# A two-layer decoder step: value half of the gated MLP by token, expert pages freed by quarters, a seventh state buffer

## The chip, the core and the metric

The kernel runs on one core of one Trainium2 chip. The metric is the device time in microseconds of one execution, from the first instruction to the last; lower is better. The time before is the median of three runs, 1581.47 us (1578.85 to 1586.49). A profiled execution gives the rows that are read below.

## What is computed

One inference step over 256 prompt tokens and 32 sample tokens (8 requests of 4), so 288 tokens in all, in float32. Layer 0 mixes tokens with an mLSTM block (a matrix memory of 4 heads for each request), layer 1 with a gated MLP whose gate is a causal 128-token spatial product; each is followed by a mixture of 32 experts with two experts for each token. Cut to what matters here:

```python
# mLSTM, for each request b and head h (8 x 4 = 32 sample states, 512 x 512 each)
c_new = decay[..., None, None] * c_prev + jnp.einsum('bhld,bhlv->bhdv', wk, v)

# gated MLP of layer 1; x is normalised first
zz = jax.nn.gelu(x @ p['cmlp_w_in'][j] + p['cmlp_b_in'][j])   # 1024 -> 4096
u, v = jnp.split(zz, 2, axis=-1)                              # 2048 each
v = layer_norm(v, p['cmlp_ln_w'][j], p['cmlp_ln_b'][j])       # over the 2048 features
mixed = jnp.einsum('gts,bcsgd->bctgd', ws, vp) + bias         # over tokens, 8 groups
return (u * mixed) @ p['cmlp_w_out'][j] + p['cmlp_b_out'][j], v

# experts, for each of 32: 1024 -> 512 gate and up, 512 -> 1024 down
a = jnp.einsum('td,edf->tef', x, p['moe_w_gate'][i, g])
b = jnp.einsum('td,edf->tef', x, p['moe_w_up'][i, g])
hg = jax.nn.silu(a) * b * combine[:, g, :, None]
y = y + jnp.einsum('tef,efd->td', hg, p['moe_w_down'][i, g])
```

## The kernel before

The program is written out by hand, engine by engine, with semaphores; nothing reorders it. TensorE is fed by `pe`, VectorE by `dve`, ScalarE by `act`, and almost all transfers are issued in order by the SyncE queue, `sp`: a wait in that queue holds back every transfer behind it. The big SBUF tensor `arena` holds ten slots of 2 MB (`pool10`), of which six form the `ring` that the dense weights use. A float32 product shows as two TensorE instructions in the trace; a transpose shows as one.

**States.** The 32 sample states of 1 MB each are loaded (`load_state`, L343), updated in place by VectorE (L1848), and stored (L396). Six half slots of the ring hold them (`cview`). In the loop at L393 to L406, `sp` stores state q as soon as it is updated, then waits until state q - 1 has landed in HBM, and then loads state q + 5 into the place that became free. When no state is left to load, the freed slots take the weights of the next projection, `z` (`load_z`): `z0` after store 27, `z1` after store 29, `z2` after store 31. TensorE reads each state in L1299, updates it through L1308, and begins `z` (L974) when everything of the last head is done and `z0` has landed.

**Experts.** Each layer runs 8 quads of four experts, each quad in two halves of two experts. The weights are pages of 2 MB, 24 for each turn of two quads: `gate`, `gate`, `up`, `up`, `down`, `down`, four times (`load_page`, L448). Ten slots take them in the order of `PAGE_SLOT`. Pages 0 to 9 are loaded ahead of the first product; page n from 10 on reuses the slot of page n - 10 (of page n - 6 from 20 on) and waits until the product that read it is done. So pages 10 to 13 wait for the end of the first `gate_up` (L1400, semaphore `gu_mm` at 1), pages 14 and 15 for the first `outputs` (L1431, `y_mm` at 1), pages 16 to 19 for the second `gate_up` (`gu_mm` at 2), and so on. `quad` sets the order of TensorE: `gate_up`, `hidden`, `outputs`, the gather of the next quad (L1374), the second `gate_up`, `hidden`, `outputs`.

**Gated MLP.** `dense("in", ...)` computes 32 tiles of 128 features by 288 tokens (L974): 16 of the value half, then 16 of the u half, 8 products each. VectorE scales each by the norm of the token (`in_scaled`, L2088), ScalarE applies the gelu with the bias of the feature (L876). The value half is needed by token, so after tiles 5, 9, 13 and 17 TensorE transposes four tiles back (`v_by_token`, L1581), VectorE copies them and takes their statistics (`values`), and after tiles 20, 22 and 24 normalises them (`layer_norm`). The spatial products (`mix`, L1536 and L1538) start behind tile 27, three for each tile, and VectorE gates u with them (`mixed`). The spatial weights are transposed once (L1570).

## Time and profile before

| | us |
|---|---|
| median of 3 runs | 1581.47 |
| lowest, highest | 1578.85, 1586.49 |
| the profiled execution | 1583.27 |
| its span, first to last instruction | 1581.5 |
| TensorE matmul busy in it | 1315.9 (83%) |
| VectorE, ScalarE busy | 510.5 (32%), 191.5 (12%) |
| moved by DMA | 532.97 MB, mean 337 GB/s |

The span falls into stretches: the up projection until about 95 us, the states until 290, `z` and `down` until 430, routing and the experts of layer 0 until 890, the gated MLP and its output until 1110, routing and the experts of layer 1 until the end. A busy share over the whole span mixes them; each stretch has its own limit. The chain of waits tells, going back from the last instruction, which work released which; the timeline of the SyncE queue tells when each transfer was issued, and the table of transfers how long it took to land.

### The profile page before, as it was taken

To read this page: it belongs to the slowest core of one execution; us is meant where nothing else is said; L and a number is where in the kernel's file an instruction comes from. 1 tells how busy PE (TensorE), PEld (TensorE's weight loads), DVE (VectorE), ACT (ScalarE), POOL (GpSimd) and SP (SyncE) were. 2 spreads that over 40 slices of the span, in tenths; PEclk is the share of its full clock that TensorE was granted. 3 is DMA by queue.
4 is the path that set the end of the run, shared out by engine and by line. 5 is a ranking of instruction groups with operands and counts; after the bars stand their busy time and mean duration, and the time that the engine had idled before them with its cause. 6 is when DMAs were issued, how large, how long until landed. Compare 5 with 4: busy or idle time off the path is not lost.

```text
span 1581.5 us, 18294 instructions
## 1 busy us (share of the span) xinstructions
PE 1315.9 (83%) x7577; PEld 734.7 (46%) x7579; DVE 510.5 (32%) x1187; ACT 191.5 (12%) x425; POOL 39.3 (2%) x78
## 2 busy tenths in 40 slices
PE   9999999999999486586585899999997757756766
PEld 6664443577654242242242577777543323323323
DVE  5757776432042022022021133630422212211212
ACT  2252221200110000000000312100200000000001
POOL 4120000000000000000000000000000000000000
PEclk9999999999999897898898999999998888888889
DMA  7228999958549999999999955361599999999996
GB/s 238 104 93 331 388 400 393 335 178 342 203 180 428 428 427 428 428 428 428 428 428 425 395 207 198 128 257 62 209 429 426 428 428 428 427 430 428 426 430 281
DMA packets 78120, 532.97 MB, mean 337 GB/s; under 512 B 6697, under 2 KB 24297, under 8 KB 43945
## 3 DMA queue, kind: packets, MB, share of 16 engines
q1 hardware_dynamic: 75112, 527.14, 81.9%
q10 hardware_dynamic: 2312, 4.20, 0.7%
q8 instruction: 52, 0.85, 0.2%
q0 software_dynamic: 624, 0.62, 0.2%
q14 instruction: 20, 0.16, 0.0%
HBM read 492.45 MB, written 39.49 MB: 336 GB/s over the span
## 4 chain that ended last, share of the span: by engine, by line
PE 58%; DMA 33%; DVE 5%; issue 2%; SPq 1%; ACT 1%; DVEq 0%
DMA arena<-in_moe_w_up 29%; PE bank L974 24%; PE bank L1400 10%; PE bank L1431 5%; PE bank L1444 3%; DMA arena<-in_moe_w_down 2%; PE bank L1374 2%; PE bank L1115 2%; PE bank L1299 1%; PE bank L1308 1%; PE bank L1408 1%; DVE arena L1848 1%; SPq L448 1%; PE bank L1100 1%; DMA out_C_s<-arena 1%
## 5 line engine op out<-in xcount | busy, mean ns | idle before, releaser
L1400 PE MATMUL bank<-arena,hT 128*32 128x512 f32 x2048 | 270.0, 687 | 193.8 <-DMA arena<-in_moe_w_up 183.6
L974 PE MATMUL bank<-hT,arena 128*128 128x288 f32 x1024 | 259.1, 411 | 0.0
L1400 PEld LDWEIGHTS bank<-arena,hT 128*32 128x32 f32 x2048 | 75.8, 124 | 375.7 <-issue 375.2
L974 PEld LDWEIGHTS bank<-hT,arena 128*128 128x128 f32 x1024 | 192.8, 191 | 56.8 <-issue 2.4
L1998 DVE TENSOR_TENSOR arena<-arena,bank 64x512 f32<-64x512 f32 x32 | 22.1, 692 | 545.9 <-ACT arena L837 545.9
L1431 PE MATMUL bank<-arena 128*32 128x512 f32 x1024 | 133.2, 664 | 21.6 <-DVE arena L2002 20.6
L1374 PE MATMUL bank<-arena 128*128 128x128 f32 (+1 forms) x768 | 136.8, 308 | 1.2 <-DVE arena L1973 0.9
L974 PE MATMUL bank<-arena 128*128 128x288 f32 x512 | 127.9, 409 | 0.0
L1374 PEld LDWEIGHTS bank<-arena 128*128 128x128 f32 (+1 forms) x768 | 104.3, 187 | 43.4 <-issue 12.7
L974 PEld LDWEIGHTS bank<-arena 128*128 128x128 f32 x512 | 96.1, 190 | 30.8 <-issue 3.5
L837 ACT ACTIVATE arena<-bank 64x512 f32<-64x512 f32 x32 | 18.8, 588 | 744.4 <-PE bank L1400 744.4
L1848 DVE SCALAR_TENSOR_TENSOR arena<-arena,bank 128x512 f32<-128x512 f32 x128 | 86.6, 740 | 34.7 <-PE bank L1308 34.6
L1431 PEld LDWEIGHTS bank<-arena 128*32 128x32 f32 x1024 | 38.9, 120 | 90.1 <-issue 89.8
L1444 PE MATMUL bank<-arena 128*128 128x288 f32 x240 | 65.9, 418 | 4.7 <-DVE xT L2031 3.9
L1991 DVE TENSOR_TENSOR hT<-bank,gpk 128x512 f32<-128x512 f32 x32 | 22.1, 691 | 117.3 <-PE bank L1374 117.3
L1444 PEld LDWEIGHTS bank<-arena 128*128 128x128 f32 x240 | 43.1, 189 | 33.3 <-issue 13.4
L1408 PE MATMUL bank<-ident,arena 64*128 64x64 f32 x256 | 35.6, 279 | 24.0 <-DVE arena L1998 22.9
L2031 DVE TENSOR_TENSOR xT<-xT,bank 128x288 f32<-128x288 f32 x120 | 52.0, 452 | 10.4 <-PE bank L1444 6.4
L1408 PEld LDWEIGHTS bank<-ident,arena 64*128 64x128 f32 x256 | 31.0, 188 | 44.1 <-DVE arena L1998 37.4
L1299 PE MATMUL bank<-arena 128*32 128x512 f32 x256 | 35.9, 633 | 5.0 <-DMA arena<-in_state_mlstm_C 4.9
L2088 DVE TENSOR_TENSOR arena<-bank,arena 128x288 f32<-128x288 f32 x32 | 14.6, 456 | 70.0 <-PE bank L974 70.0
L1308 PE MATMUL bank<-arena 32*128 32x512 bf16 x128 | 35.1, 392 | 0.6 <-ACT arena L716 0.4
(367 smaller groups left out, 991.0 us busy)
## 6 DMA issues: line engine op xcount, KB each, us to landing
arena<-in_moe_w_gate SPq DMA_DIRECT2D x64, 2048.0 KB, 29.2
arena<-in_moe_w_up SPq DMA_DIRECT2D x60, 2048.0 KB, 33.4
arena<-in_moe_w_down SPq DMA_DIRECT2D x60, 2048.0 KB, 25.4
arena<-in_state_mlstm_C SPq DMA_DIRECT2D x32, 1024.0 KB, 8.5
out_C_s<-arena SPq DMA_DIRECT2D x32, 1024.0 KB, 10.9
arena<-in_cmlp_w_in SPq DMA_DIRECT2D x8, 2048.0 KB, 17.9
arena<-in_mlstm_w_up SPq DMA_DIRECT2D x7, 2048.0 KB, 9.9
arena<-in_mlstm_w_down SPq DMA_DIRECT2D x4, 2048.0 KB, 18.4
```

The costliest lines, as they stand in the source:

```text
L974: ins = mm(B[m % 4][:, 0:NT], w[:, k, 128 * i:128 * i + 128], rhs(k), start=(k == 0), stop=(k == kt - 1))
L1115: ins = mm(B[state_bank(h, i)][:, :], wks[h % 2][:, j, 128 * i:128 * i + 128], values_of(h, j), start=(j == 0), stop=(j == 1))
L1299: mm(B[4][NS * i:NS * i + NS, :], qz[:, i, NS * b:NS * b + NS], cview(q)[:, i, :], start=(b == 0), stop=(b == NB - 1), skip_group_check=True)
L1308: mm(B[UPD[n % 4]][:, :], wk8[g:g + 32, b // 4, 128 * i:128 * i + 128], v8[g:g + 32, b // 4, :], start=True, stop=True).then_inc(s("c_mm"), 1)
L1374: ins = mm(B[6 + k // 4][:, QUAD * (k % 4):QUAD * (k % 4) + QUAD], rows_of(j)[:, 128 * k:128 * k + 128], sel[0:t, buf, j, :], start=(j == ...
L1400: ins = mm(B[j][CAP * i:CAP * i + CAP, :], xq[h][:, k, CAP * e:CAP * e + CAP], w[i][:, k, :], start=(k == 0), stop=(k == KD - 1), skip_gro ...
L1408: ins = mm(B[2][:, 256 * j + 64 * f:256 * j + 64 * f + 64], sg[64:P, j, 128 * f:128 * f + 128], ident[64:P, 64:P], start=True, stop=True)
L1431: ins = mm(B[4 + c][r:r + CAP, :], hxT[:, j, 64 * f + CAP * e:64 * f + CAP * e + CAP], w[e][:, f, 512 * c:512 * c + 512], start=(f == 0), ...
L1444: mm(B[SCATTER[m % 3]][:, 0:NT], ysb[:, m // 4, 128 * (m % 4):128 * (m % 4) + 128], wpair[:, buf, m // 4, :], start=True, stop=True).then_ ...
L1848: stt(c, c, decb[:, h, b:b + 1], B[UPD[n % 4]][:, :], ALU.mult, ALU.add).then_inc(s("c_new"), 1)
L1991: tt(xq[buf][:, 4 * c:4 * c + 4, :], B[6 + c][:, :].rearrange("p (k c) -> p k c", k=4), gpk[:, L, 4 * c:4 * c + 4].unsqueeze(2).to_broadca ...
L2031: tt(xT[:, m, :], xT[:, m, :], B[SCATTER[m % 3]][:, 0:NT], ALU.add).then_inc(s("moe_add"), 1)
```

## The change

Three edits.

1. **A seventh state.** State 6 gets a buffer of its own (`extra_state`), where the folded query blocks `bda` lie until the last query product. It is loaded ahead of the loop, once all 16 query products are done. States 7 and up move down by one buffer (`buffer_of`). In the loop, store r is followed by load r + 7 for r below 6, by none for r = 6, and by load r + 6 after that. The z weights follow stores 28, 30 and 31 in the place of 27, 29 and 31. The head outputs `hhp` are laid out in the other direction, so that those that share the place come last.
2. **Pages by quarters.** Pages 10 to 13 of each layer's first turn are loaded in three parts of a quarter, a quarter and a half. The first `gate_up` counts after k = 1 and k = 3 of its 8 steps (`pe_part`), and each part is issued when the rows of the old pages that it overwrites have been read.
3. **Value half by token.** The value half is computed with the tokens on the partitions: 8 tiles of 128 tokens by 512 features, and the 32 sample tokens as four products side by side in the columns of the array. VectorE scales by the token's norm (now a number for each partition, `crstd`) and adds the bias (`vbias`, loaded for all partitions), ScalarE applies the gelu in place. The transposes and copies back are gone. The order of the loads around it changes with it.

```diff
+PARTS = ((0, 4), (4, 8), (8, 16))
+VT = 12
+EXTRA = 6
...
-        hhp = [at(arena, after + h * 1024, 2, DH) for h in range(H)]
+        hhp = [at(arena, after + (3 - h) * 1024, 2, DH) for h in range(H)]
+        extra_state = at(arena, after, MH, DH)
...
+            sp.wait_ge(s("q_mm"), KI)
+            load_state(EXTRA)
             for q in range(NB * H + 1):
...
-                    if r + 6 < NB * H:
-                        load_state(r + 6)
-                    elif r % 2 == 1:
-                        load_z((r - 27) // 2)
+                    ahead = r + 7 if r < EXTRA else r + 6
+                    if r != EXTRA and ahead < NB * H:
+                        load_state(ahead)
+                    elif r in (28, 30, 31):
+                        load_z((28, 30, 31).index(r))
...
-                for n in range(PAGES):
+                for n in range(10):
+                    load_page(n, 0, 0, first=True)
+                for part, (k0, k1) in enumerate(PARTS):
+                    if part < 2:
+                        sp.wait_ge(s("pe_part"), 1 + 2 * L + part + 1)
+                    else:
+                        sp.wait_ge(s("gu_mm"), base * 4 + 1)
+                    for n in range(10, 14):
+                        slot, dst = expert_page(n)
+                        a = (gate, gate, up, up, down, down)[n % 6][L * NE + n // 6 * 2 + n % 2]
+                        unit = 4 if n % 6 >= 4 else 2
+                        sp.dma_start(dst[:, k0 // unit:k1 // unit, :], a[:, k0 // unit:k1 // unit, :]) \
+                            .then_inc(s(f"expert_landed{slot}"), 16)
+                for n in range(14, PAGES):
                     load_page(n, 0, 0, first=True)
...
-                    sp.wait_ge(s("in_mm"), 4 * (j - 5))
+                    sp.wait_ge(s("in_mm"), 9)
...
                     sp.wait_ge(s("moe_add"), last * (2 * KD) + 2 * KD)
+                    sp.dma_start(vbias, A["cmlp_b_in"][:, INNER:2 * INNER].to_broadcast([P, INNER])).then_inc(s("ws_landed"), 16)
                     sp.dma_start(raw_ws, A["cmlp_w_s"][0].rearrange("g t s -> t g s")).then_inc(s("ws_landed"), 16)
...
+                        if first and k in (1, 3):
+                            ins.then_inc(s("pe_part"), 1)
                     ins.then_inc(s("gu_mm"), 1)
...
+            for n in range(8):
+                c, j = divmod(n, 2)
+                t0 = TOK[j][0]
+                if j == 0:
+                    landed(pe, "in", c)
+                if n >= 4:
+                    pe.wait_ge(s("in_scaled"), n - 3)
+                for k in range(KD):
+                    if n == 0:
+                        pe.wait_ge(s("hg"), k + 1)
+                    ins = mm(B[n % 4][:, :], hT[:, k, t0:t0 + P], page8(c)[:, k, :], start=(k == 0), stop=(k == KD - 1))
+                ins.then_inc(s("in_mm"), 1)
...
+            pe.wait_ge(s("ws_out"), 2)
+            for k in range(KD):
+                for c in range(4):
+                    ins = mm(B[4][NS * c:NS * c + NS, :], hT[:, k, 256:NT], page8(c)[:, k, :],
+                             start=(k == 0), stop=(k == KD - 1), skip_group_check=True)
+            ins.then_inc(s("in_mm"), 1)
+            for m in range(KI):
+                if m % 4 == 0:
+                    landed(pe, "in", 4 + m // 4)
+                pe.wait_ge(s("in_scaled"), 5 + m if m < 4 else VT + m - 3)
...
-            def v_by_token(m):
...
+            def value_scaled(n):
+
+                j, c = (n % 2, n // 2) if n < 8 else (2, n - 8)
+                dve.wait_ge(s("in_mm"), min(n, 8) + 1)
...
+                stt(value_tile(n), src[0][:, :], src[1], src[2], ALU.mult, ALU.add).then_inc(s("in_scaled"), 1)
```

The order of the transfers on the SyncE queue at the end of the states (`in_mlstm_w_up` is a z page). Before:

```order
L343 DMA arena<-in_state_mlstm_C 128x2048 [waits s_c_stored1]
L396 DMA out_C_s<-arena 128x2048 [waits s_c_new]
L396 DMA out_C_s<-arena 128x2048 [waits s_c_new,s_c_stored0]
L329 DMA arena<-in_mlstm_w_up 128x8x512 [waits s_c_stored1]
L396 DMA out_C_s<-arena 128x2048 [waits s_c_new]
L396 DMA out_C_s<-arena 128x2048 [waits s_c_new,s_c_stored0]
L329 DMA arena<-in_mlstm_w_up 128x8x512 [waits s_c_stored1]
```

And of the changed kernel:

```order
L361 DMA arena<-in_state_mlstm_C 128x2048 [waits s_c_stored1]
L416 DMA out_C_s<-arena 128x2048 [waits s_c_new]
L416 DMA out_C_s<-arena 128x2048 [waits s_c_new,s_c_stored0]
L416 DMA out_C_s<-arena 128x2048 [waits s_c_new,s_c_stored1]
L346 DMA arena<-in_mlstm_w_up 128x8x512 [waits s_c_stored0]
L416 DMA out_C_s<-arena 128x2048 [waits s_c_new]
L416 DMA out_C_s<-arena 128x2048 [waits s_c_new,s_c_stored1]
```

The first z page stands one store later in the queue, behind store 29 and the landing of store 28.

On the same queue, at the first product of the experts of layer 0. Before:

```order
L448 DMA arena<-in_moe_w_up 128x4096 [waits s_down_mm] x2
L448 DMA arena<-in_moe_w_down 128x4096 [waits s_gu_mm] x2
L448 DMA arena<-in_moe_w_gate 128x4096 [waits s_gu_mm] x2
L448 DMA arena<-in_moe_w_up 128x4096 [waits s_y_mm] x2
L448 DMA arena<-in_moe_w_down 128x4096 [waits s_gu_mm] x2
```

And of the changed kernel:

```order
L469 DMA arena<-in_moe_w_up 128x4096 [waits s_down_mm] x2
L482 DMA arena<-in_moe_w_down 128x1024 [waits s_pe_part]
L482 DMA arena<-in_moe_w_down 128x1024
L482 DMA arena<-in_moe_w_gate 128x1024 x2
L482 DMA arena<-in_moe_w_down 128x1024 [waits s_pe_part]
L482 DMA arena<-in_moe_w_down 128x1024
L482 DMA arena<-in_moe_w_gate 128x1024 x2
L482 DMA arena<-in_moe_w_down 128x2048 [waits s_gu_mm]
L482 DMA arena<-in_moe_w_down 128x2048
L482 DMA arena<-in_moe_w_gate 128x2048 x2
L469 DMA arena<-in_moe_w_up 128x4096 [waits s_y_mm] x2
L469 DMA arena<-in_moe_w_down 128x4096 [waits s_gu_mm] x2
```

Four loads that waited for the whole product have become twelve, of which eight wait for a part of it; what follows waits for the same products as before.

TensorE in the value half of the gated MLP (L974 is a tile, L902 the sum of squares, L1570 the spatial weights, L1581 the transposes back). Before:

```order
L974 MATMUL bank<-hT,arena 128x288 [waits s_hg] x7
L902 MATMUL bank<-arena,ones 128x288 [waits s_sq,s_moe_add]
L974 MATMUL bank<-hT,arena 128x288 x24
L974 MATMUL bank<-hT,arena 128x288 [waits s_in_scaled,s_page_landed1]
L1570 MATMUL bank<-ident,arena 128x128 [waits s_ws_landed,s_std]
L1581 MATMUL bank<-ident,arena 128x128 [waits s_gelu,s_ws_out]
L974 MATMUL bank<-hT,arena 128x288 [waits s_in_scaled]
L1581 MATMUL bank<-ident,arena 128x128 [waits s_vtk,s_gelu]
```

And of the changed kernel (L1600 is a value tile, L1609 and L1611 the norms by token, L1622 the sample tokens, L1630 a u tile):

```order
L1600 MATMUL bank<-arena,hT 128x512 [waits s_hg] x7
L1609 MATMUL bank<-ones,arena 128x1 [waits s_std]
L1611 MATMUL bank<-ones,arena 32x1 x4
L1600 MATMUL bank<-arena,hT 128x512 [waits s_page_landed1]
L1600 MATMUL bank<-arena,hT 128x512 [waits s_in_scaled,s_page_landed2]
L1616 MATMUL bank<-ident,arena 128x128 [waits s_ws_landed]
L1622 MATMUL bank<-arena,hT 32x512 [waits s_ws_out]
L1622 MATMUL bank<-arena,hT 32x512 x31
L1630 MATMUL bank<-hT,arena 128x288 [waits s_in_scaled,s_page_landed4]
```

The transposes and their waits for the gelu are gone, the spatial weights are transposed after the fifth value tile, and the wait for them to be copied (`ws_out`) has moved to the sample products.

## Rows read from the trace of the kernel before

**Rows 1.** The page's chain that ended last: shares of the span by line.

```profile
DMA arena<-in_moe_w_up 29%; PE bank L974 24%; PE bank L1400 10%; PE bank L1431 5%; PE bank L1444 3%; DMA arena<-in_moe_w_down 2%; PE bank L1374 2%; PE bank L1115 2%; PE bank L1299 1%; PE bank L1308 1%; PE bank L1408 1%; DVE arena L1848 1%; SPq L448 1%; PE bank L1100 1%; DMA out_C_s<-arena 1%
```

**Rows 2.** Stretches: us, busy of PE, PEld, DVE, ACT, POOL, clock, DMA share, GB/s.

```profile
100.00:120.00 20.00, 19.49 (x169) 13.48 (x168) 15.02 (x36) 14.65 (x40) 8.45 (x17) 1.00 0.10 29
140.00:260.00 120.00, 117.65 (x602) 47.15 (x594) 87.48 (x192) 33.11 (x66) 5.69 (x17) 1.00 1.00 393
470.00:880.00 410.00, 286.43 (x1976) 131.92 (x1972) 77.75 (x191) 15.84 (x28) 0.00 (x0) 0.86 1.01 428
925.00:1045.00 120.00, 120.00 (x548) 95.06 (x546) 60.91 (x109) 17.16 (x31) 0.55 (x1) 1.00 0.40 134
```

**Rows 3.** The chain in order of time, states to z: start, us, what.

```profile
269.85 9.08 DMA arena<-in_state_mlstm_C
...
292.32 15.52 PE bank L974 x64
```

**Rows 4.** SyncE's timeline at the end of the states: start, us, line, transfer, count.

```profile
270.24 6.50 SPq L396 DMA_DIRECT2D out_C_s<-arena  x2
281.41 0.39 SPq L329 DMA_DIRECT2D arena<-in_mlstm_w_up  x1
```

**Rows 5.** What SyncE waited for: us in total, times, longest.

```profile
SPq L343 <- DMA out_C_s<-arena: 109.3, 25, 5.6
...
SPq L396 <- DVE arena L1848: 44.6, 15, 26.1
```

**Rows 6.** Landing of two issues, store 28 (276.40) and z0 (281.41): KB, us.

```profile
out_C_s<-arena SPq DMA_DIRECT2D x1, 1024.0 KB, 7.4
...
arena<-in_mlstm_w_up SPq DMA_DIRECT2D x1, 2048.0 KB, 9.9
```

**Rows 7.** The chain in order of time: first expert product of layer 0.

```profile
452.81 7.00 PE bank L1400 x64
```

**Rows 8.** SyncE's timeline behind that product: pages 10, 14 and 16.

```profile
459.87 0.81 SPq L448 DMA_DIRECT2D arena<-in_moe_w_down  x2
...
471.46 0.80 SPq L448 DMA_DIRECT2D arena<-in_moe_w_up  x2
486.92 0.81 SPq L448 DMA_DIRECT2D arena<-in_moe_w_down  x2
```

**Rows 9.** Landing of the issues at 459.87 and 486.92: KB, us.

```profile
arena<-in_moe_w_down SPq DMA_DIRECT2D x1, 2048.0 KB, 7.9
...
arena<-in_moe_w_down SPq DMA_DIRECT2D x1, 2048.0 KB, 11.5
```

**Rows 10.** SyncE's timeline in layer 1: pages 10 and 16.

```profile
1140.34 0.81 SPq L448 DMA_DIRECT2D arena<-in_moe_w_down  x2
...
1166.98 0.80 SPq L448 DMA_DIRECT2D arena<-in_moe_w_down  x2
```

**Rows 11.** Groups by line, 893 to 1046 us: busy us, mean ns, idle before.

```profile
L974 PE MATMUL bank<-hT,arena 128*128 128x288 f32 x512 | 126.5, 407 | 0.0
...
L1581 PE MATMUL bank<-ident,arena 128*128 128x128 f32 (+1 forms) x48 | 6.0, 274 | 0.9 <-DVE arena L2094 0.9
```

**Rows 12.** TensorE's timeline: the first transposes back, and the idle time before.

```profile
922.95 1.53 PE L1581 MATMUL bank<-ident,arena 128*128 128x128 f32 x12 [0.94 <-DVE arena L2094]
```

**Rows 13.** SyncE's timeline at the spatial weights and their bias.

```profile
894.49 5.12 SPq L476 DMA_DIRECT2D arena<-in_cmlp_w_s  x1
899.65 5.29 SPq L477 DMA_DIRECT2D arena<-in_cmlp_b_s  x1
```

**Rows 14.** Landing of these two: KB, us.

```profile
arena<-in_cmlp_w_s SPq DMA_DIRECT2D x1, 512.0 KB, 13.6
arena<-in_cmlp_b_s SPq DMA_DIRECT2D x1, 512.0 KB, 11.5
```

**Rows 15.** Groups by line, 115 to 292 us: one of VectorE, one of TensorE.

```profile
L1848 DVE SCALAR_TENSOR_TENSOR arena<-arena,bank 128x512 f32<-128x512 f32 x128 | 86.6, 740 | 34.7 <-PE bank L1308 34.6
...
L1115 PE MATMUL bank<-arena 128*128 128x512 f32 x64 | 32.7, 637 | 0.0
```

## Prediction before the result

> **What bounds the kernel now.** Start with the page's chain [rows 1]: the largest share is the landing of expert pages, 29%, the next TensorE on the dense weights, 24%. So the limit changes by stretch, and the stretches come second [rows 2]. From 470 to 880 us the 16 DMA engines are full at 428 GB/s while TensorE is busy 286 of 410 us: there only an earlier start of the stream can bring the end forward. From 925 to 1045 us it is the reverse: TensorE is busy all 120 us at full clock (2.4 GHz) and the DMA share is 0.40: there only TensorE work counts. From 140 to 260 us both are nearly full (TensorE 117.7 of 120, DMA 1.00 at 393 GB/s), after 20 us in which the DMA share was 0.10. Third, for each of the three places, SyncE's timeline with the landing times, because it shows which wait ends last.
>
> The sum is made against the profiled execution, 1583.27 us (span 1581.5 and 1.8 around it), which lies 1.8 above the median of 1581.47. What it saves is then taken from the median.
>
> **Part 1, the pages by quarters.** Before, pages 10 to 13 are issued at 459.87, when the first product ends (452.81 + 7.00) [rows 7, 8], into an empty queue: the first lands 7.9 later at 467.8 [rows 9]. A page is 2.1 MB, 4.9 us at 428 GB/s [rows 2], so data flow from about 3.0 us after an issue into an idle queue, and page 13 lands at 467.8 + 3 x 4.9 = 482.5. Pages 14 and 15 (issued 471.46) follow without a gap until 492.3 to 493.5; page 16 is issued at 486.92 and lands at 498.4, 11.5 later, so it had queued for 3.6 of these [rows 8, 9].
>
> With quarters the first part leaves after 2 of 8 steps, at 452.81 + 1.75 = 454.6, the second at 456.3, the last at 459.8. The stream begins 5.25 us earlier, and each part (2.1 MB, 4.9 us) covers the wait for the next. Pages 10 to 13 are down by 477.3, pages 14 and 15 (issued at 471.46, 5.8 before that, against 3.0 needed) by 487.1. Here the head start meets its limit: page 16 still waits for the second product, and TensorE's path to it has no transfer in it. Issued at 486.92 into a queue that is drained, it lands 7.9 later at 494.8 in the place of 498.4. So **3.6 us of the 5.25 remain**, and a hole of some 2 us appears in the stream. Behind it the queue is ahead again (pages 20 and 21 are asked for at 502.3, pages 16 to 19 land until 509.5), so the 3.6 hold to the end of the layer, which the full stretch to 880 carries [rows 2]. Layer 1 repeats it: from page 10 to page 16 are 1140.34 to 1166.98, 26.6 us, against 27.05 in layer 0 [rows 8, 10]; with the same landings that is 3.5. **Sum 7.1 us**, from 0 (the start is lost at the hole) to 10.5 (all of it is kept). SyncE issues eight loads more a layer, each 0.4 us [rows 8], while it would wait anyway; behind its new waits stand only loads that wait for later products.
>
> **Part 2, the value half.** In the gated MLP TensorE has no gap but 0.94 us [rows 11, 12], so its work is counted. Removed: 16 tiles of 16 instructions at 15.52 / 64 = 0.2425 us each [rows 3], 62.1; the transposes, 6.0 less the overlap of their four groups, 5.3; the 0.94 of waiting for the spatial weights, whose copy will lie under three value tiles. In all 68.3. Added: 8 tiles of 16 instructions over 512 columns. No row shows these in a long run; by columns from the 288-wide ones each is 0.2425 x 512 / 288 = 0.431, 55.2 in all. The nearest row of the same width, L1115, has 32.7 / 64 = 0.51 [rows 15], but in short groups with an ending each, and would give 65.4. I take 55.2, as the 288-wide tiles run back to back in the same loop. Then 64 instructions of the sample tokens, four to a step in separate 32-column strips, the form of the expert product: 7.0 [rows 7]. And 12 tiny ones for the norms, at most the 0.125 of a transpose [rows 11], 1.0. In all 63.2, so **5.1 us are saved**, with bounds from -5.1 to 6.
>
> The strips are where I looked for a rule against the change. The row says that they run side by side: 64 x 0.431 = 27.6 would be the price one after another, and 7.0 is a quarter of it. The Trainium skill, page "TensorE: Matmul & The Clock Gate", part 3 (Packing small matmuls), measured only 3.07 times for four row tiles and 2.38 for three column tiles. By that the samples would take 9.0 to 11.6 and the whole kernel 2.0 to 4.6 us more; the row decides.
>
> What could uncover this work: VectorE has a 128 x 512 pass of 0.74 for each tile of 6.9 us [rows 15] and loses 16 scalings and 12 copies. Its first pass now waits for three loads. Before, the last of them lands at 899.65 + 11.5 = 911.2 [rows 13, 14]; the broadcast bias puts 1 MB more ahead, 2.6 us at 393 GB/s, and perhaps one more issue as slow as its neighbours' 5.1 to 5.3, so 914 to 917. TensorE needs the pass at its fifth tile, at 894 + 4 x 6.9 + 3.9 (the sum of squares, 16 instructions) + 1 = 926.5. Nothing waits. The last value pages serve until the samples are done, so the u pages 6 and 7 leave only then; they are due 31 us later, eight tiles on, and land after 8 to 13. The end of the stretch (spatial products from the twelfth u tile) stands to the u tiles as before.
>
> **Part 3, the seventh state.** The states' queue is transfer-bound: SyncE waited 25 times, 109 us, for a store to land before it could load, and 14 times, only 18.5 us, for an update once the first is past [rows 5]. One load of 1.05 MB fewer is 2.7 us at 393 GB/s; some of it goes where stores wait for updates. I take 2.3 (1.0 to 2.7) for the last load, which lands at 269.85 + 9.08 = 278.9, and after which TensorE needs 13.4 us until z at 292.32 [rows 3]. But z0 landed at 281.41 + 9.9 = 291.3, only 1.0 before that [rows 4, 6], and is now issued one store later: behind store 28, which landed at 276.40 + 7.4 = 283.8, and with store 29 ahead of it in the queue, 2.5 to 2.7. So z0 lands at 291.3 - 2.3 + 2.5 = 291.5 and becomes the last wait: **0.8 us are saved**, from -0.5 (the stream gains 1.0) to 2.3 (store 29 doesn't delay it). Behind z TensorE runs without a transfer's wait to the expert product, so this passes on whole. Load 6 itself costs nothing: it falls in the 20 us with a DMA share of 0.10 [rows 2].
>
> **Sum.** 7.1 + 5.1 + 0.8 = 13.0: 1583.27 becomes 1570.3, and the median **1568.5 us**, 0.8% below.
>
> **The rivals.**
> - **Wide products pay L1115's price.** At 0.478 to 0.51 a piece the value half takes 61 to 65 and part 2 gives -1 to -5: about 1575.5. For it: the only 512-wide full-array row. Against it: that row's groups of four instructions. 10%.
> - **The head start is lost,** the change not doing what it says: the hole before page 16 becomes as long as the start was early, should the refill after a drained queue take 3.6 us more than the 7.9 shown. 1575.6. Against it: both layers show the same 7.9 and 11.5 pattern. 8%.
> - **Everything is kept**: the second product comes earlier too, 10.5, and z0 doesn't wait, 2.3: 1563.6. Against it: the 27 us to the second product hold no transfer. 11%.
> - **Slower: the pieces don't queue.** If each of the eight quarter loads takes its own turn, about 3.1 us, pages 10 to 13 take 8 x 3.1 + 9.8 = 34.6 in the place of 19.6, 15.0 more against the 5.25 of the earlier start: the stream is 9.8 later in each layer. With parts 2 and 3 kept that is 1581.5 - 5.9 + 19.6 = 1595. It decides from 2.3 us a piece on, where two layers lose the 5.9. For it: the 512 KB of the bias land 911.2 - 908.1 = 3.1 us after those of the weights [rows 13, 14]. Against it: that load was issued 5 us late, and the DMA engines stayed full meanwhile. 5%. The Trainium skill, page "DMA: Bandwidth & Descriptors", section Bandwidth, has the rule that speaks for it: batch to 1 MiB or more; no row here shows quarter pages in a queue.
>
> **How the numbers follow.** The forecast has 63%; rivals as given, 3% for what I don't see. The range reaches over the third rival's neighbourhood and to the first two: 1562 to 1577, with the slower rival outside. A measurement of this kernel can tell about 0.5% (7.9 us) from no change: faster is the forecast and the third rival with part of the rest, 0.78; within 0.5% are the first two, mostly, 0.15; slower 0.07.
>
> **What would show it.** The first quarter issued 1.75 us after the first product starts, and page 16 landing about 8 us after its issue, behind a short hole in the DMA share, in both layers. Value tiles at 6.9 us with no gap before the fifth, samples at 7 us, u tiles as before. TensorE waiting for `in_mlstm_w_up` ahead of z. I am wrong if value tiles take over 7.5 us, if page 16 lands as late after the first product as before (38.6 us), or if z moves forward by more than 2 us.

## The result and the profile after

The changed kernel takes **1578.62 us** (median of 20 executions, 1569.47 to 1591.57), the kernel before 1587.16 in the same sitting (20 executions, 1578.85 to 1594.02). The ratio is 0.9942, 95% interval 0.9925 to 0.9959: 9.2 us faster, 6.5 to 11.9. The forecast was 13.0 us faster, at 1568.5 with a range of 1562 to 1577. So the sign was right, the gain too large by two fifths, and the time lies 1.6 us outside the range. Taken as a difference the range was 4.5 to 19.5 us faster, and the 9.2 lie in it. Much of the distance in the time itself is the level: the three executions on which the forecast stands had a median of 1581.47, and the 116 executions of the kernel before that were timed in all have a mean of 1586.6 and reach from 1577.4 to 1600.8. 0.9942 times 1581.47 would have been 1572.3.

The profiled execution of the changed kernel took 1580.41 us (span 1578.7). Its chain names the same limits as [rows 1], with the shares by line:

```profile
DMA arena<-in_moe_w_up 29%; PE bank L1012 17%; PE bank L1443 10%; PE bank L1476 5%; PE bank L1630 4%; PE bank L1600 3%; PE bank L1489 2%; PE bank L1415 2%; PE bank L1153 2%; DVE arena L1907 2%; PE bank L1340 1%; PE bank L1453 1%; PE bank L1349 1%; DMA arena<-in_moe_w_down 1%; SPq L469 1%
```

Two of the stretches of [rows 2], the experts of layer 0 and the gated MLP (us, busy of PE, PEld, DVE, ACT, POOL, granted clock, DMA share, GB/s):

```profile
470.00:880.00 410.00, 290.62 (x1965) 132.88 (x1968) 82.27 (x204) 15.85 (x28) 0.00 (x0) 0.86 1.01 426
897.90:1043.60 145.70, 145.70 (x583) 92.25 (x581) 62.03 (x106) 25.27 (x47) 1.64 (x2) 1.00 0.56 194
```

The DMA engines are as full as before in the first, and TensorE works without a gap in the second, at a granted clock of 1.00 (2.4 GHz).

**The pages by quarters.** SyncE's timeline in layer 0 (start, us, line, transfer, count): the three parts of pages 10 to 13 (L482), then pages 14, 16 and 20 (L469), to be read beside [rows 8].

```profile
459.74 0.80 SPq L482 DMA_DIRECT2D arena<-in_moe_w_down  x2
...
461.53 1.22 SPq L482 DMA_DIRECT2D arena<-in_moe_w_down  x2
...
464.89 0.90 SPq L482 DMA_DIRECT2D arena<-in_moe_w_down  x2
...
476.48 0.80 SPq L469 DMA_DIRECT2D arena<-in_moe_w_up  x2
491.93 0.81 SPq L469 DMA_DIRECT2D arena<-in_moe_w_down  x2
...
507.30 0.80 SPq L469 DMA_DIRECT2D arena<-in_moe_w_up  x2
```

The landing of the first quarter (459.74), of page 16 in layer 0 (491.93) and of page 16 in layer 1 (1167.27), beside [rows 9] (KB, us):

```profile
arena<-in_moe_w_down SPq DMA_DIRECT2D x1, 512.0 KB, 4.0
...
arena<-in_moe_w_down SPq DMA_DIRECT2D x1, 2048.0 KB, 8.0
...
arena<-in_moe_w_down SPq DMA_DIRECT2D x1, 2048.0 KB, 7.6
```

The first product starts at 457.75, so the first part leaves 1.99 us later; page 16 lands 8.0 after its issue, at 499.95. Both are what the forecast asked for.

**The value half.** Groups by line, 897.5 to 1044 us, beside [rows 11] (busy us, mean ns, idle before): the u tiles, the value tiles, the sample tokens, the sum of squares.

```profile
L1630 PE MATMUL bank<-hT,arena 128*128 128x288 f32 x256 | 63.7, 408 | 0.0
L1600 PE MATMUL bank<-arena,hT 128*128 128x512 f32 x128 | 55.7, 593 | 0.0
...
L1622 PE MATMUL bank<-arena,hT 128*32 128x512 f32 x64 | 7.1, 594 | 0.0
...
L940 PE MATMUL bank<-arena,ones 128*128 128x288 f32 x16 | 4.0, 406 | 0.0
```

Eight value tiles in 55.7 us (55.2 forecast) and the samples in 7.1 (7.0): the terms of the sum stand.

**The states.** The chain in order of time at the end of the states, beside [rows 3] (start, us, what), with the issue of `z0` by SyncE and its landing, beside [rows 4, 6]:

```profile
286.36 3.63 PE bank L1153 x8
289.99 3.72 issue
293.71 17.45 PE bank L1012 x64
```

```profile
284.34 0.39 SPq L346 DMA_DIRECT2D arena<-in_mlstm_w_up  x1
```

```profile
arena<-in_mlstm_w_up SPq DMA_DIRECT2D x1, 2048.0 KB, 9.3
```

TensorE waits 3.72 us for `z0`, which lands at 293.62, and then its first 64 instructions of `z` take 17.45 us, where [rows 3] have 15.52. The wait was forecast, the second thing was not.

Nor was the length of the wait. TensorE is ready for `z` 10.7 us after the last state has landed, where the forecast has 13.4. Before, it ran that stretch at the half clock: its products with the last state, and the window behind them (columns as above); then the same products here.

```profile
278.98 1.94 PE L1299 MATMUL bank<-arena 128*32 128x512 f32 x8 [2.02 <-DMA arena<-in_state_mlstm_C]
```

```profile
279.00:286.00 7.00, 7.00 (x17) 1.23 (x18) 2.79 (x5) 0.60 (x1) 0.00 (x0) 0.53 0.78 286
```

```profile
279.33 1.06 PE L1340 MATMUL bank<-arena 128*32 128x512 f32 x8
```

### The profile page after: what moved, and what is told of

It is laid out like the page before. It is cut to its first block, busy times and chain, and to the rows that moved or that the text cites. A ratio compares the mean times of both kernels' runs of the same rounds, so it can differ in the third digit from the quotient of the medians.

```text
span 1578.7 us, 18090 instructions
## 1 busy us (share of the span) xinstructions
PE 1315.3 (83%) x7477; PEld 714.1 (45%) x7479; DVE 502.8 (32%) x1172; ACT 190.7 (12%) x421; POOL 39.9 (3%) x78
## 4 chain that ended last, share of the span: by engine, by line
PE 59%; DMA 31%; DVE 5%; issue 2%; SPq 1%; ACT 1%; DVEq 0%; POOL 0%; POOLq 0%
DMA arena<-in_moe_w_up 29%; PE bank L1012 17%; PE bank L1443 10%; PE bank L1476 5%; PE bank L1630 4%; PE bank L1600 3%; PE bank L1489 2%; PE bank L1415 2%; PE bank L1153 2%; DVE arena L1907 2%; PE bank L1340 1%; PE bank L1453 1%; PE bank L1349 1%; DMA arena<-in_moe_w_down 1%; SPq L469 1%
## 5 line engine op out<-in xcount | busy, mean ns | idle before, releaser
L1443 PE MATMUL bank<-arena,hT 128*32 128x512 f32 x2048 | 264.2, 674 | 194.3 <-DMA arena<-in_moe_w_up 176.4
L1476 PE MATMUL bank<-arena 128*32 128x512 f32 x1024 | 136.3, 678 | 20.9 <-DVE arena L2061 20.7
L1012 PE MATMUL bank<-hT,arena 128*128 128x288 f32 x512 | 136.6, 424 | 3.7 <-issue 3.7
L1012 PEld LDWEIGHTS bank<-hT,arena 128*128 128x128 f32 x512 | 98.7, 197 | 36.1 <-issue 6.4
L1476 PEld LDWEIGHTS bank<-arena 128*32 128x32 f32 x1024 | 40.4, 122 | 91.3 <-issue 91.0
L1630 PE MATMUL bank<-hT,arena 128*128 128x288 f32 x256 | 63.7, 408 | 0.0
L1489 PEld LDWEIGHTS bank<-arena 128*128 128x128 f32 x240 | 43.1, 189 | 33.3 <-issue 13.4
L1600 PE MATMUL bank<-arena,hT 128*128 128x512 f32 x128 | 55.7, 593 | 0.0
L1630 PEld LDWEIGHTS bank<-hT,arena 128*128 128x128 f32 x256 | 48.1, 190 | 13.9 <-issue 0.8
## 6 DMA issues: line engine op xcount, KB each, us to landing
arena<-in_moe_w_down SPq DMA_DIRECT2D x12, 1024.0 KB, 14.5
```

The source lines that it names most:

```text
L1012: ins = mm(B[m % 4][:, 0:NT], w[:, k, 128 * i:128 * i + 128], rhs(k), start=(k == 0), stop=(k == kt - 1))
L1443: ins = mm(B[j][CAP * i:CAP * i + CAP, :], xq[h][:, k, CAP * e:CAP * e + CAP], w[i][:, k, :], start=(k == 0), stop=(k == KD - 1), skip_gro ...
L1476: ins = mm(B[4 + c][r:r + CAP, :], hxT[:, j, 64 * f + CAP * e:64 * f + CAP * e + CAP], w[e][:, f, 512 * c:512 * c + 512], start=(f == 0), ...
L1489: mm(B[SCATTER[m % 3]][:, 0:NT], ysb[:, m // 4, 128 * (m % 4):128 * (m % 4) + 128], wpair[:, buf, m // 4, :], start=True, stop=True).then_ ...
L1600: ins = mm(B[n % 4][:, :], hT[:, k, t0:t0 + P], page8(c)[:, k, :], start=(k == 0), stop=(k == KD - 1))
L1630: ins = mm(B[m % 4][:, 0:NT], page8(4 + m // 4)[:, k, 128 * (m % 4):128 * (m % 4) + 128], hT[:, k, :], start=(k == 0), stop=(k == KD - 1))
```

## How the experiments are read

Single executions of one kernel scatter by some 4.7 us (standard deviation). Much of it goes with the TensorE clock: over the 20 executions of the changed kernel the mean granted clock and the time have a correlation of -0.87 (0.922 with 1569.9, 0.910 with 1591.6), over the 116 of the kernel before -0.71. So each gain below is a difference of means over all timed executions, with a 95% interval, against those 116 of the kernel before, and beside it stand the lengths of the stretches in the profiles, which scatter far less where the DMA queue or a gapless TensorE sets them. Each column adds up to the span of its profile, but for rounding:

| us | before | states alone | quarters alone | value alone, twice | changed, twice | second product too, twice | both additions |
|---|---|---|---|---|---|---|---|
| start to the first state's load | 55.9 | 55.9 | 57.7 | 57.2, 56.9 | 60.4, 55.9 | 57.5, 60.3 | 56.1 |
| first state's load to the last landing | 223.0 | 223.7 | 222.7 | 228.2, 223.0 | 218.9, 215.9 | 217.5, 223.0 | 220.9 |
| last landing to `z` | 13.2 | 14.4 | 12.1 | 14.3, 12.4 | 14.4, 14.6 | 15.1, 14.5 | 17.3 |
| `z` to the first product | 160.6 | 163.4 | 160.7 | 162.3, 162.3 | 164.0, 163.7 | 162.4, 160.7 | 162.3 |
| first product to the last page, layer 0 | 434.3 | 434.3 | 432.8 | 434.0, 434.1 | 431.9, 432.0 | 430.7, 430.9 | 430.4 |
| last page to the gated MLP | 6.8 | 6.8 | 6.8 | 6.8, 6.8 | 8.3, 8.0 | 8.3, 6.8 | 6.8 |
| gated MLP | 151.2 | 151.2 | 151.2 | 145.7, 145.7 | 145.7, 145.7 | 145.7, 145.7 | 145.7 |
| output projection to the first product | 88.2 | 88.2 | 88.2 | 93.0, 88.2 | 88.2, 88.2 | 88.2, 88.2 | 88.2 |
| first product to the last page, layer 1 | 434.2 | 434.1 | 432.8 | 435.4, 433.7 | 432.6, 432.6 | 430.5, 430.8 | 430.3 |
| last page to the end | 14.2 | 15.4 | 15.4 | 15.5, 15.4 | 14.2, 14.2 | 14.2, 14.2 | 14.2 |

## Experiments: each edit alone

**The seventh state alone** (edit 1 on the kernel before):

```diff
+            sp.wait_ge(s("q_mm"), KI)
+            load_state(EXTRA)
...
-                    elif r % 2 == 1:
-                        load_z((r - 27) // 2)
+                    elif r in (28, 30, 31):
+                        load_z((28, 30, 31).index(r))
```

> The seventh state alone, the rest as before. If the three edits simply add up: 0.5 to 1.5 us faster, as forecast (0.8), with TensorE waiting up to 1 us for the first z page. If what the whole change lacks was lost here: 2 to 4 us slower, because TensorE stands some 4 us ahead of z for the page that is now issued behind store 28, and goes on at the half clock behind that wait.

1584.06 us median of 12, ratio 0.9990 (0.9969 to 1.0011); mean gain 1.2 +- 2.6. The pause (4.20 us) and the slow start of `z` are there (+1.2 and +2.8 us in the table), but the kernel is not the 2 to 4 us slower of the second theory.

**The quarters alone** (edit 2):

```diff
-                for n in range(PAGES):
+                for n in range(10):
                     load_page(n, 0, 0, first=True)
+                for part, (k0, k1) in enumerate(PARTS):
...
```

> The pages by quarters alone. If the edits add up: 7 us faster, with page 16 landing 35 us after the end of the first product's wait in the place of 38.6 in layer 0 and the same in layer 1. If the head start is given back behind page 16 (the hole there, and TensorE at the half clock in the last products of layer 0): 3 to 4 us faster, with page 16 as early as that and the last page of the layer less early.

1582.82 us median of 12, ratio 0.9984 (0.9960 to 1.0008); mean gain 3.2 +- 2.8. The last page of each layer lands 1.5 and 1.3 us earlier after the first product: the gain is that of the second theory, and it is lost in the page stream itself.

**The value half alone** (edit 3), run twice:

```diff
-            dense("in", 8, 4, 512, KD, lambda k: hT[:, k, :], "in_mm", lambda m: pe.wait_ge(s("in_scaled"), m + 1),
+            for n in range(8):
+                c, j = divmod(n, 2)
...
```

> The value half by token alone. If the edits add up: 5.1 to 5.5 us faster, all of it between the first product of the gated MLP and the output projection, and nothing elsewhere. If the shorter gated MLP leaves TensorE waiting for the first expert pages of layer 1, or the earlier loads disturb the last pages of layer 0: 2 to 3 us faster, with the gated MLP itself as short.

1587.74 us median of 12, ratio 0.9995 (0.9970 to 1.0020), though its gated MLP is 5.5 us shorter. In this profile the gather ahead of the first product of layer 1 (TensorE's timeline) ran at a granted clock of 0.60 on average, then 0.50 (windows, columns as above):

```profile
1127.69 13.83 PE L1386 MATMUL bank<-arena 128*128 128x128 f32 x48 [0.41 <-DVE arena L1999]
```

```profile
1128.40:1138.40 10.00, 9.93 (x37) 7.58 (x38) 2.28 (x13) 0.00 (x0) 0.00 (x0) 0.60 0.37 156
1138.40:1141.40 3.00, 3.00 (x11) 2.15 (x10) 0.00 (x0) 0.00 (x0) 0.00 (x0) 0.50 0.00 0
```

It took 9.01 us in the profile of before. TensorE's pauses in the 10 us ahead of it are of at most 0.6 us, as they are in the profile of before, so this is no wait of the change's making. That profile also has 5.2 us more in the stretch of the states, where this edit changes nothing.

> The value half by token alone, once more, as its first timing showed no gain though its gated MLP took 145.7 us in the place of 151.2. If that timing was scatter: 4 to 6 us faster than before, with the stretch from the output projection to the first product of layer 1 at 88.2 us as in every other trace. If the single edit loses its gain at the half clock in the gather of layer 1: no gain again, and that stretch at 93 us.

1583.24 us median of 12, ratio 0.9977 (0.9951 to 1.0002), and the stretch is back at 88.2. The stretch is that of the first theory; the mean gain of this timing, 2.9 +- 3.4, decides for neither. Both timings together: 1.0 +- 2.5.

**All three, on the same chip**, the same kernel as in the result:

> The changed kernel again, beside the three single edits on the same chip. If the edits add up, its gain is the sum of theirs within 2.5 us; if they take from each other (one makes another's wait the last), it is 3 us or more below the sum. About 9 us faster either way.

1575.68 us median of 8, ratio 0.9929 (0.9900 to 0.9958). With the first 20 executions the mean gain is 9.2 +- 2.1. The single edits add to 5.4 +- 4.6, so the changed kernel is not held back by its edits taking from each other; if anything it is the other way.

## Experiments: each edit left out

The same hunks, with one edit's taken away:

**Without the seventh state,** run twice:

> The changed kernel without the seventh state: quarters and value half by token. If the seventh state is worth the 2 us that its single edit showed: 2 us slower than the changed kernel, the first four tiles of z at 15.6 us, the value half as short as in the changed kernel (145.7 us), together about 8 us faster than before. If the value half by token gains nothing in the end, as its single edit showed: 4 us faster than before.

> The changed kernel without the seventh state, once more. If the pause and the slow first tiles of z take back what the shorter stream of the states brings: within 2 us of the changed kernel. If the edit is worth the 2 us of its single timing: 2 to 3 us slower than the changed kernel.

1576.51 (10 executions) and 1577.87 (6): ratios 0.9940 (0.9902 to 0.9977) and 0.9945 (0.9926 to 0.9965). The means are 0.8 +- 3.1 us *below* the changed kernel: on top of the other two, the seventh state is worth nothing that shows. Against the kernel before the two others gain 10.0 +- 2.5, so the value half does not come to nothing in the end.

**Without the quarters:**

> The changed kernel without the quarters: seventh state and value half by token. By what the traces show of the quarters (the last page of a layer 2 us earlier in layer 0, 1.4 us in layer 1): 3 to 4 us slower than the changed kernel, about 6 us faster than before. If the value half gains only together with the quarters: within 2 us of before.

1578.28 us median of 12, ratio 0.9963 (0.9940 to 0.9985); the quarters are worth 2.7 +- 2.7 on top of the others. First product to last page: 434.6 and 434.3, as before.

**Without the value half:**

> The changed kernel without the value half: seventh state and quarters, gated MLP as before (151.2 us). If the value half is worth what its stretch shows: 5 to 6 us slower than the changed kernel, 3 to 5 us faster than before. If it is worth only what its single edit gained: 1 to 2 us slower than the changed kernel, 7 to 8 us faster than before.

1582.68 us median of 12, ratio 0.9980 (0.9959 to 1.0002). The value half is worth 5.4 +- 3.2 on top of both others, 5.3 +- 3.1 on top of the states, 6.7 +- 3.6 on top of the quarters, and 1.0 +- 2.5 alone. Three of the four are near the 5.5 of its stretch.

With these all eight combinations of the three edits are timed. The mean over the four pairs that differ in one edit alone is 4.6 +- 1.6 for the value half, 4.3 +- 1.6 for the quarters (3.2 alone, 2.6 on the states, 2.7 on both, 8.9 on the value half) and 1.6 +- 1.6 for the seventh state (1.2 alone, 0.6 on the quarters, -0.8 on both, 5.5 on the value half). The three that stand apart, 1.0, 8.9 and 5.5, all rest on one kernel, the value half alone.

## Experiments: where the quarters' gain goes

Landing of pages after the start of the first product, from the transfers' own issue and landing times, layer 0 and layer 1:

| us | page 13 | page 15 | page 16 issued | page 16 | page 21 |
|---|---|---|---|---|---|
| before | 29.8, 30.6 | 40.8, 40.4 | 34.2, 33.8 | 45.7, 45.3 | 70.2, 69.7 |
| changed | 26.0, 26.7 | 35.9, 36.5 | 34.2, 35.4 | 42.2, 43.0 | 67.7, 68.6 |
| second product too | 26.1, 26.7 | 36.2, 36.6 | 30.3, 30.3 | in pieces | 66.6, 66.5 |

On TensorE's path to the second product of layer 1, the first `outputs` before and in the changed kernel:

```profile
1146.53 4.94 PE L1431 MATMUL bank<-arena 128*32 128x512 f32 x32 [0.71 <-DVE arena L2002]
```

```profile
1145.83 5.93 PE L1476 MATMUL bank<-arena 128*32 128x512 f32 x32 [0.71 <-DVE arena L2061]
```

**Pages 16 to 19 by quarters too:**

```diff
-                for n in range(14, PAGES):
+                for n in range(14, 16):
                     load_page(n, 0, 0, first=True)
+                for part, (k0, k1) in enumerate(PARTS):
+                    if part < 2:
+                        sp.wait_ge(s("pe_part"), 1 + 4 * L + part + 3)
+                    else:
+                        sp.wait_ge(s("gu_mm"), base * 4 + 2)
+                    for n in range(16, 20):
...
-                    gate_up(q, turn, h, 1)
+                    gate_up(q, turn, h, 1, first=first)
```

> The changed kernel, with pages 16 to 19 freed by quarters too, behind the steps of the second product. If the head start is given back in the hole ahead of page 16 and in the uneven landings behind it (1.4 to 1.8 us and about 1.1 us a layer): pages 16 to 21 follow page 15 at 4.9 us each, the last page of each layer lands 1.5 to 2.7 us earlier than in the changed kernel, and the kernel is 3 to 5 us faster. If small loads cost the queue as much as the hole (the quarters of pages 10 to 13 took 1.6 us more than their bytes need): under 1 us is gained.

> The changed kernel with pages 16 to 19 by quarters, once more, beside the one with the small products ahead of z. Last pages 1.2 to 2.2 us earlier a layer than in the changed kernel, 1572 to 1574 us, 3 to 5 us faster than the changed one; if the few runs of the first timing were luck: 1576 us or more.

1571.56 us (median of 4) and 1576.16 (6), ratios 0.9897 (0.9832 to 0.9963) and 0.9922 (0.9892 to 0.9952). Together 3.1 +- 2.7 us faster than the changed kernel. SyncE's timeline of layer 0, the pages 16 and 17 in their three parts (L495) where the first product starts at 452.45:

```profile
482.72 0.80 SPq L495 DMA_DIRECT2D arena<-in_moe_w_down  x2
...
484.52 1.58 SPq L495 DMA_DIRECT2D arena<-in_moe_w_down  x2
...
487.87 0.80 SPq L495 DMA_DIRECT2D arena<-in_moe_w_down  x2
```

The landing of the first piece and of page 20 and 21:

```profile
arena<-in_moe_w_down SPq DMA_DIRECT2D x1, 512.0 KB, 7.2
...
arena<-in_moe_w_up SPq DMA_DIRECT2D x2, 2048.0 KB, 13.2
```

The first piece lands 1.3 us after page 15, so the hole is gone, and page 21 lands 1.2 and 2.1 us earlier than in the changed kernel. The gain is where the first theory put it, at the lower end of its sizes.

## Experiments: the first z page

**`z0` in two halves,** behind stores 27 and 28:

```diff
-                    elif r in (28, 30, 31):
-                        load_z((28, 30, 31).index(r))
+                    elif r in (27, 28):
+                        k = 4 * (r - 27)
+                        load("z", 0, w_up[:, k:k + 4, 2048:2560], k8(page("z", 0))[:, k:k + 4, :])
+                    elif r in (30, 31):
+                        load_z(r - 29)
```

> The changed kernel, with the first z page loaded in two halves: the first behind store 27, the second behind store 28. If the wait for that page and the slow first tiles behind it cost what the traces show (1.2 us from the last state to z, 3 us in the first four tiles of z at 0.48 us an instruction): the page lands 1.5 to 2.5 us earlier, TensorE waits about 2 us in the place of 4, the first four tiles take 15.5 to 17 us in the place of 17.4 to 18.8, and the kernel is 2 to 4 us faster than the changed one. If the page is bound by the full queue: it lands within 0.5 us of before, and nothing is gained.

1581.71 us median of 10, ratio 0.9961 (0.9925 to 0.9997): not faster than the changed kernel. The second half, issued at 279.40 as soon as store 28 is down, takes 12.2 us, for half the bytes that took 9.3; two stores stand around it in the queue, and store 29 lands only after 10.3. TensorE then waits 6.75 us:

```profile
arena<-in_mlstm_w_up SPq DMA_DIRECT2D x1, 1024.0 KB, 12.2
```

```profile
291.68 17.68 PE L1017 MATMUL bank<-hT,arena 128*128 128x288 f32 x64 [6.75 <-issue]
```

Nothing is gained, as the second theory has it, but its mechanism is not borne out either: the page is down 17.1 us after the last state, not within 0.5 of the 14.3 and 14.5 of the changed kernel. Why the half took longer than a page is not settled.

**Small products while TensorE waits:**

```diff
+            pe.wait_ge(s("c_new"), 32 * H - 3)
+            keep_busy(UPD[0], 14)
             dense("z", 4, 4, 512, KD, lambda k: hT[:, k, :], "z_mm", lambda m: pe.wait_ge(s("zs"), m + 1),
```

> The changed kernel, with 14 small products on TensorE while it waits for the first z page (3.2 us, their result is not used). If the slow first tiles come from the pause ahead of them: the first four tiles of z take 15.5 us in the place of 17.4 to 18.8, z itself begins within 0.5 us as before, and the kernel is 2 to 3 us faster. If they are slow for another reason (the page's last bytes, the output stores): they stay at 17 to 19 us, and nothing changes or up to 1 us is lost.

1579.49 us median of 10, ratio 0.9954 (0.9915 to 0.9993). TensorE's timeline in three kernels (start, us, line; in brackets the idle time before): the changed kernel in its second profile, this one, and the one without the quarters, which happened to wait only 1.59 us.

```profile
286.38 18.80 PE L1012 MATMUL bank<-hT,arena 128*128 128x288 f32 x64 [4.33 <-issue]
```

```profile
296.47 3.21 PE L949 MATMUL bank<-onesb 128*128 128x512 bf16 x14
299.52 15.68 PE L1012 MATMUL bank<-hT,arena 128*128 128x288 f32 x64
```

```profile
287.35 15.76 PE L998 MATMUL bank<-hT,arena 128*128 128x288 f32 x64 [1.59 <-issue]
```

In the first of them the clock granted at the start of `z` was (windows, columns as above):

```profile
286.40:291.80 5.40, 5.40 (x12) 3.78 (x13) 4.22 (x10) 0.00 (x0) 0.22 (x3) 0.50 1.02 406
291.80:305.20 13.40, 13.40 (x56) 10.43 (x54) 0.00 (x0) 1.23 (x3) 0.00 (x0) 0.97 1.03 377
```

So the pause costs twice: `z` starts later, and its first tiles run at half the clock (0.50, 1.2 GHz), 12 instructions in 5.4 us. Over all profiles the first 64 instructions took 15.7 to 15.8 us behind a pause of 0, 0.21, 1.06, 1.59, 1.89 or 2.04 us, and 17.4 to 18.8 behind 2.75, 3.23, 3.72, 4.20, 4.33 and 6.75. With the small products in the pause they take 15.68. Without these the pause would have been some 2.7 us, as the product ahead of them ends at 296.63 and `z0` lands at 299.27. So cause and effect are shown, the filled pause in one profile. The Trainium skill, page "TensorE: Matmul & The Clock Gate", section "Why this matters for your kernels", says that long idle stretches between bursts of products bring the low clock back; these rows agree. The time of the whole kernel does not show the 2 to 3 us (2.3 +- 4.4 slower than the changed one): that is too small for ten executions of this scatter.

**Both additions,** second product by quarters and small products:

> The changed kernel with pages 16 to 19 by quarters and with small products while TensorE waits for the first z page. If both add up: 5 us from the pages (hole and uneven landings gone in both layers) and 2 to 3 us from the first four tiles of z at 15.5 us: 1569 to 1571 us, 16 us faster than before and 7 us faster than the changed kernel. If the first tiles of z count for nothing in the end, as the single timing of that edit showed: 1572 to 1574 us.

1570.90 us median of 6 (1567.7 to 1576.6), ratio 0.9896 (0.9865 to 0.9927): 15.1 +- 2.8 us faster than before and 5.9 +- 3.3 faster than the changed kernel, the fastest of all here. In its profile `z0` was down 2.7 us before `z` began, so the small products themselves held `z` back, and this profile is no test of the filled pause. Against the second product by quarters alone the gain is 2.8 +- 3.3: what the small products add to the time is not shown.

## Why the prediction was right and wrong

- **The level** failed first. "What it saves is then taken from the median" of three executions; that median lies 5 us under the mean of 116, with a scatter of 4.7 for one: two of the three lay 5 to 8 us under it. That was bad luck, but the range made no room for it.
- **Part 2, the value half (5.1 forecast): right.** 151.2 to 145.7 us, 5.5, in each of the twelve profiles that have it; value tiles 7.0 us (0.435 an instruction), samples 7.1, no gap. The 288-wide tiles, scaled by columns, and not the 0.51 of L1115 [rows 15], were the right neighbour of the wide products: the first rival falls. Four strips side by side took 7.1 us, a quarter of 64 x 0.435 = 27.8. The Trainium skill, page "TensorE: Matmul & The Clock Gate", part 3 (Packing small matmuls), has smaller factors, from which the prediction estimated 9.0 to 11.6 us; the 7.1 measured decide. The kernel's time shows it in three of four comparisons.
- **Part 1, the quarters (7.1 forecast): mis-sized.** Mechanism and sign are right; the first product to the last page is 2.0 us shorter in layer 0 and 1.9 in layer 1 (means over eight profiles with the quarters and five without), 3.8 to 3.9 in all, and the time gained 2.6 to 3.2 in three of the four pairs. Counted to the gated MLP, and to the end, the two layers gain 1.3 and 2.6: another split of about the same sum. The second and third rival fall with it: neither nothing nor all of the head start is kept. Three steps of the sum failed. First, "pages 10 to 13 are down by 477.3": page 13 lands 3.8 to 3.9 us earlier, not 5.2; the first part leaves 0.24 later than forecast, and two of its quarters in layer 0 land 1.9 us behind the one before, where queued ones take 1.25. Second, "the same landings" in layer 1: page 16 was asked for 35.4 us after the first product in the place of 33.8, because TensorE's path to the second product had run longer at the half clock (the granted clock was 0.74 from 1139 to 1152 us, and 0.85 from 1140.3 to 1152 before). The profile without the quarters has this path in both layers (35.4), so it is no work of theirs. Page 16 gained 2.3 there, 3.5 in layer 0 (3.6 forecast). Third, "the 3.6 hold to the end of the layer": between pages 16 and 21 another 1.0 to 1.2 us went, in one pair of landings 6.0 us apart in the place of 4.9, with the queue full. Quarters behind the second product brought back 1.6 to 2.0 a layer; what made single landings late is open. The fourth rival, pieces that don't queue, falls: queued quarters land about 1.25 us apart (1.24 to 1.29 for pages 16 to 19).
- **Part 3, the seventh state (0.8 forecast): about right by cancelling, which is luck.** The stream of the states is 3.5 +- 3.0 us shorter (mean of ten profiles with it against six without), so the 2.3 assumed are not refuted. `z0` lands 2.0 us later behind the last state (14.3 to 15.0 in the place of 12.0 to 13.4; 2.5 forecast), became the last wait and took about 1.5 of the gain back (last landing to `z`), as forecast. Two things were wrong. "After which TensorE needs 13.4 us until z" is a time at the half clock: where none of that stretch ran at it, TensorE was ready after 10.2 to 10.7. So `z0` was the last wait already in three of the six profiles without this edit (pauses of 0.21, 1.89 and 2.04 us), and with it TensorE waits up to 4.33. And the term that was missing is the clock behind that wait, 1.7 to 3.1 us where the pause was 2.75 or more. Gain alone 1.2 +- 2.6, on top of the others -0.8 +- 3.1. The sign "z moves forward by more than 2 us" decides nothing: `z` begins at 293.7 and 286.4 in the two profiles of the changed kernel, at 292.2 before.
- **The sum.** 5.5 for the value half, 3.8 for the pages and nothing for the state give 9.3; measured 9.2 +- 2.1. By this account the missing 3.8 us are the pages' 3.3 and the state's 0.8, less 0.4 that the value half gave more; that the two sums meet within 0.1 is chance.
- **Open:** that the value half alone gained 1.0 +- 2.5. The slow gather of layer 1 turned up in one of its two profiles, and also in one of the two without the seventh state (a stretch of 93.1 us there), a kernel that kept its gain; so it does not explain it.

## What to carry to other kernels

Size a head start at the far end of the stream, not where it begins: each later place where the queue can run dry takes a part of it, and all of these have to be opened. A wait in front of TensorE can cost its length and then the half clock behind it (here behind 2.75 us and more, not behind 2.04); price both, or fill it. Look at the granted clock of a stretch before taking a wait's margin from it: a path read at the half clock is shorter at the full one. Three executions give a level no better than their scatter: forecast the difference, and let the range hold the level as well.

## What the runs showed of the hardware

Ahead of `z`, pauses of up to 2.04 us left TensorE at the full clock. Behind those of 2.75 us and more its next instructions began at 1.2 GHz (granted clock 0.50), and the first 64 took 17.4 to 18.8 us in the place of 15.7 to 15.8. Half-clock stretches also came where TensorE had no pause of over 0.6 us (the gather of 13.83 us, in two of the sixteen profiles). They go with the scatter between executions: in the changed kernel 0.012 in the mean granted clock went with 21.7 us. A 1 MB load with stores around it in the queue took 12.2 us, longer than 2 MB behind the same stores (9.3).
